# A two-block model on one core: decay factors of the mLSTM by a split row product, four buffers, later ScalarE work, and a key strip ahead of the Hyena transforms

## The reference

```python
logw = F[..., :, None] - F[..., None, :] + ic[..., None, :]
logw = jnp.where(lower, logw, -jnp.inf)
m_t = jnp.maximum(log_inter, jnp.max(logw, axis=-1))
w = jnp.exp(logw - m_t[..., None])
s = jnp.einsum('bhtd,bhsd->bhts', qc, kc) * w
h = num / jnp.maximum(jnp.abs(den), jnp.exp(-m_t))[..., None]
```

## Time and profile before

| | us |
|---|---|
| median of 3 runs | 1810.19 |
| the profiled execution: its time | 1808.34 |
| its span in the trace | 1806.5 |
| TensorE busy with products | 1735.1 (96%) |
| VectorE, ScalarE, GpSimd busy | 877.3, 667.0, 831.5 |

### The profile page before, as it was taken

How to read it: one execution, slowest core, us unless ns; L and a number is a source line. 1 busy time by engine, 2 the same in 40 slices (tenths; PEclk the granted TensorE clock), 3 DMA queues, 4 the chain that set the end, 5 groups by cost and what they waited for, 6 DMA issues and landing times.

```text
span 1806.5 us, 21589 instructions
## 1 busy us (share of the span) xinstructions
PE 1735.1 (96%) x7584; PEld 1398.8 (77%) x7584; DVE 877.3 (49%) x1163; ACT 667.0 (37%) x850; POOL 831.5 (46%) x614
## 2 busy tenths in 40 slices
PE   7999999888998999999999999999999999999996
PEld 4677767776785888888888788888888888888885
DVE  6447666776425371424255767664333343132235
ACT  4434344434423322111124566665333432222222
POOL 4324422467540354444443666565444354444443
PEclk9999999889999999999999999999999999999998
DMA  5112211125220222222222333332222222322222
GB/s 199 59 40 89 70 48 47 70 94 175 85 92 19 97 94 93 93 95 99 97 93 93 108 102 117 105 116 93 93 102 96 94 93 95 103 93 93 104 94 93
DMA packets 47631, 168.60 MB, mean 93 GB/s; under 512 B 5141, under 2 KB 5269, under 8 KB 47322
## 3 DMA queue, kind: packets, MB, share of 16 engines
q1 hardware_dynamic: 46016, 163.75, 26.3%
q10 hardware_dynamic: 1562, 4.13, 0.6%
HBM read 165.76 MB, written 2.10 MB: 93 GB/s over the span
## 4 chain that ended last, share of the span: by engine, by line
PE 42%; issue 21%; POOL 14%; DVE 2%; POOLq 0%; ACT 0%; DMA 0%; DVEq 0%; SPq 0%
PE ps L518 14%; POOL m_w_lo L479 14%; PE ps L519 14%; PE ps L520 14%; DVE m_h L2129 0%; DVE m_ZL L1748 0%; DVE m_qs L1738 0%; DVE m_TM L1822 0%; DVE m_s L1440 0%; DMA m_raw<-in_strips 0%; DVE m_s L1818 0%; POOL m_QL L497 0%; POOLq L487 0%; DVE m_QL L1810 0%; POOLq L485 0%
## 5 line engine op out<-in xcount | busy, mean ns | idle before, releaser
L479 POOL TENSOR_TENSOR m_w_lo<-m_raw,m_w_hi 128x512 fp32r<-128x512 f32 x604 | 816.7, 1374 | 939.1 <-ACT m_w_hi L1003 939.0
L1003 ACT ACTIVATE m_w_hi<-m_raw 128x1024 fp32r<-128x1024 f32 x302 | 318.7, 1057 | 626.7 <-DMA m_raw<-in_strips 626.4
L518 PE MATMUL ps<-m_XH,m_w_hi 128*128 128x512 f32 x1096 | 440.2, 402 | 5.5 <-POOL m_w_lo L479 5.1
L520 PE MATMUL ps<-m_XH,m_w_lo 128*128 128x512 f32 x1096 | 429.4, 392 | 0.0
L519 PE MATMUL ps<-m_XL,m_w_hi 128*128 128x512 f32 x1000 | 392.1, 392 | 0.0
L518 PEld LDWEIGHTS ps<-m_XH,m_w_hi 128*128 128x128 f32 x1096 | 207.6, 189 | 59.5 <-issue 10.4
L520 PEld LDWEIGHTS ps<-m_XH,m_w_lo 128*128 128x128 f32 x1096 | 207.3, 189 | 43.8
L519 PEld LDWEIGHTS ps<-m_XL,m_w_hi 128*128 128x128 f32 x1000 | 189.7, 190 | 40.5 <-issue 2.0
L518 PE MATMUL ps<-m_FH,m_w_hi 128*128 128x512 f32 x432 | 168.3, 390 | 0.3 <-DVE m_FL L1433 0.3
L519 PE MATMUL ps<-m_FL,m_w_hi 128*128 128x512 f32 x432 | 168.2, 389 | 0.0
L520 PE MATMUL ps<-m_FH,m_w_lo 128*128 128x512 f32 x432 | 168.2, 389 | 0.0
(11 more groups left out here) (335 smaller groups left out, 2289.4 us busy)
## 6 DMA issues: line engine op xcount, KB each, us to landing
m_raw<-in_strips SPq DMA_DIRECT2D x302, 512.0 KB, 3.2
m_x_in<-in_x SPq DMA_DIRECT2D x4, 512.0 KB, 11.8
m_x_res<-in_x ACTq DMA_DIRECT2D x1, 2048.0 KB, 8.3
out<-m_h SPq DMA_DIRECT2D x8, 256.0 KB, 2.2
m_decay<-in_decay ACTq DMA_DIRECT2D x1, 1024.0 KB, 10.4
m_memf<-in_mem SPq DMA_DIRECT2D x1, 1024.0 KB, 16.5
m_w<-in_w ACTq DMA_DIRECT2D x1, 512.0 KB, 8.1
m_const<-in_const ACTq DMA_DIRECT2D x1, 256.0 KB, 6.9
```

The lines of the kernel that those rows point to most:

```text
L479: nc.gpsimd.tensor_tensor(w_lo[:, c], raw[:, c], f(w_hi[:, c]), ALU.subtract).then_inc(lo_ready, 1)
L518: pe.matmul(dst, w_hi[:, c], xh, start=first, stop=False)
L520: return pe.matmul(dst, w_lo[:, c], xh, start=False, stop=last)
L1003: act.activation(w_hi[:, c], raw[:, c], ACT.Copy).then_inc(hi_ready, 1)
```

## The change

The row -M is split into a rounded part `gMH` (ScalarE) and the rest `gML` (VectorE), the selector is copied to fp32r (`sel_r`), and `row` becomes two fp32r products instead of one fp32 product. The exponential is one instruction, read from PSUM with a as the bias; where the mask applies its value may exceed 1, and VectorE's product with the triangle becomes a minimum. There are four buffers instead of two. ScalarE's `ahead`, `keep` and `out_squares` come two or three steps later in its order. Column copies and the denominator are done in fewer instructions. The first key strip is stored, loaded and used ahead of the first transform strip, and two key strips' work is placed around `back`.

```diff
-HY_STRIPS = ((S_HY, S_HY + 5, S_HY + 6, S_HY + 7), tuple(range(S_HY + 12, S_HY + 16)))
-K_STRIPS = tuple(range(S_HY + 1, S_HY + 5)) + tuple(range(S_HY + 8, S_HY + 12))
+HY_STRIPS = ((S_HY + 1, S_HY + 5, S_HY + 6, S_HY + 7), tuple(range(S_HY + 12, S_HY + 16)))
+K_STRIPS = (S_HY,) + tuple(range(S_HY + 2, S_HY + 5)) + tuple(range(S_HY + 8, S_HY + 12))
...
+        ex = [s0, s1, at("ex2", T, 116 * KB), at("ex3", T, 118 * KB)]
@@ -676,15 +681,18 @@
-            pe.wait_ge(ld_sel, 16)
+            pe.wait_ge(g_high, 2)
+            pe.wait_ge(g_low, 1)
...
                 if unit:
-                    pe.wait_ge(m_arg, TT * unit)
+                    pe.wait_ge(m_exp, TT * unit)
                 hd, d = divmod(unit, 2)
-                pe.matmul(ps[:, 5, :], sel[0:4, hd * P:(hd + 1) * P], gM[0:4, d * T:(d + 1) * T],
-                          start=True, stop=True).then_inc(m_row, 1)
+                for part in (gMH, gML):
+                    mm = pe.matmul(ps[:, 5, :], sel_r[0:4, hd * P:(hd + 1) * P], part[0:4, d * T:(d + 1) * T],
+                                   start=part is gMH, stop=part is gML)
+                mm.then_inc(m_row, 1)
@@ -803,17 +811,18 @@
+            pe.wait_ge(evac, E_WOUT)
+            pe.wait_ge(mem_ready, KT)
+            keys(0)
             pe.wait_ge(z_ready, 2)
             pe.wait_ge(m_w, STEPS)
-            pe.wait_ge(evac, E_WOUT)
-            pe.wait_ge(mem_ready, KT)
             forward(0, 0)
             forward(0, 1)
-            keys(0)
             keys(1)
             pe.wait_ge(y_ready, 1)
-            back(12, 0)
+            back(12, 0, (0, 1))
             keys(2)
+            back(12, 0, (2, 3))
             keys(3)
@@ -1171,6 +1180,9 @@
             act.activation(gE[0:4, :], gE[0:4, :], ACT.Exp, scale=-1.0).then_inc(g_em, 1)
+            act.activation(gMH[0:4, :], gM[0:4, :], ACT.Copy).then_inc(g_high, 1)
+            act.wait_ge(ld_sel, 16)
+            act.activation(sel_r[0:4, :], sel[0:4, :], ACT.Copy).then_inc(g_high, 1)
             for u in range(1, N_QK):
                 ahead(S_QK + u)
...
+            def behind(n):
+                for m in range(1, N_Z):
+                    if m > 2 and first_step(m * KT + 1) == n - 3:
+                        ahead(S_Z + m)
+                    if m < N_Z - 2 and first_step(m * KT + 16) == n - 4:
+                        keep(m)
+                if n > 2 * TT and n % (2 * TT) == 7:
+                    out_squares(n // (2 * TT) - 1)
...
             for n in range(STEPS):
...
-                if n >= 2:
-                    act.wait_ge(m_w, n - 1)
-                act.activation(e, ps[:, 5, causal(n)], ACT.Relu, bias=misc[:, c:c + 1], scale=-1.0).then_inc(m_arg, 1)
-                act.wait_ge(m_arg, n + 1)
-                act.activation(e, e, ACT.Exp, scale=-1.0).then_inc(m_exp, 1)
-                if n > 2 * TT and n % (2 * TT) == 4:
-                    out_squares(n // (2 * TT) - 1)
-                for m in range(1, N_Z):
-                    if m > 2 and first_step(m * KT + 1) == n - 1:
-                        ahead(S_Z + m)
-                    if m < N_Z - 2 and first_step(m * KT + 16) == n - 1:
-                        keep(m)
+                if n >= 4:
+                    act.wait_ge(m_w, n - 3)
+                act.activation(ex[n % 4][:, causal(n)], ps[:, 5, causal(n)], ACT.Exp, bias=misc[:, c:c + 1]
+                               ).then_inc(m_exp, 1)
+                behind(n)
+            for n in range(STEPS, STEPS + 4):
+                behind(n)
...
+            act.wait_ge(m_w, STEPS)
             keep(N_Z - 2)
@@ -1638,6 +1656,9 @@
             for u in range(1, N_QK):
                 qk_convolved(u)
+                if u == 1:
+                    dve.wait_ge(g_high, 1)
+                    dve.tensor_tensor(gML[g, :], gM[g, :], f(gMH[g, :]), ALU.subtract).then_inc(g_low, 1)
...
-            dve.tensor_scalar(misc[:, 0:32], ps[:, 7, 0:32], -1.0, None, ALU.mult).then_inc(g_colsv, 1)
-            dve.tensor_copy(misc[:, 32:64], ps[:, 7, 32:64]).then_inc(g_colsv, 1)
+            dve.tensor_copy(misc[:, 0:64], ps[:, 7, 0:64]).then_inc(g_colsv, 1)
...
-                ch.add(dve.tensor_tensor(e[:, c], e[:, c], tri[d], ALU.mult))
+                ch.add(dve.tensor_tensor(e[:, c], e[:, c], tri[d], ALU.min))
...
-                ch.add(dve.tensor_copy(den, raw_den))
-                ch.sync()
-                ch.add(dve.scalar_tensor_tensor(den, den, -1.0, den, ALU.mult, ALU.max))
-                ch.sync()
-                ch.add(dve.tensor_tensor(den, den, misc[:, 32 + d * 16 + hd:48 + d * 16:4], ALU.max))
+                ch.add(dve.tensor_tensor(den, raw_den, misc[:, 32 + d * 16 + hd:48 + d * 16:4], ALU.max))
+                ch.sync()
+                ch.add(dve.scalar_tensor_tensor(den, raw_den, -1.0, den, ALU.mult, ALU.max))
...
+                if d == 0:
+                    r = inv.rearrange("p (a c) -> p a c", c=1).to_broadcast([P, TT, P])
+                    ins = dve.tensor_tensor(acc[:].rearrange("p (a c) -> p a c", a=TT), num[:, :, 0:P], r, ALU.mult)
```

More of the change, by code:

```diff
@@ L210, in build @@
         sel = at("sel", 4 * P, 192 * KB + 3584)
+        sel_r = at("sel_r", 4 * P, 192 * KB + 3584, F32R)
+        gMH = at("gMH", 2 * T, 112 * KB, F32R)
+        gML = at("gML", 2 * T, 42 * KB, F32R)
         ZH = at("ZH", TT * T, 136 * KB + 128, F32R)
@@ L354, in build @@
         g_em = sem("g_em")
+        g_high = sem("g_high")
+        g_low = sem("g_low")
         g_cols = sem("g_cols")
@@ L358, in build @@
         m_row = sem("m_row")
-        m_arg = sem("m_arg")
         m_exp = sem("m_exp")
@@ L695, in outputs @@
                 else:
-                    pe.wait_ge(g_colsv, 2)
+                    pe.wait_ge(g_colsv, 1)
                 for tt in range(TT):
@@ L720, in _, with back @@
             z_turn(N_Z - 1)
-            def back(first, count0):
-                for q in range(4):
+            def back(first, count0, qs=range(4)):
+                for q in qs:
                     b = 6 + q % 2
@@ L1195, in _ @@
             ahead(S_Z + 2)
-            act.wait_ge(g_colsv, 2)
+            def behind(n):
[6 more added lines that the diff above has]
+                    out_squares(n // (2 * TT) - 1)
+            act.wait_ge(g_colsv, 1)
             for n in range(STEPS):
@@ L1665, in _ @@
             dve.wait_ge(g_cols, 1)
-            dve.tensor_scalar(misc[:, 0:32], ps[:, 7, 0:32], -1.0, None, ALU.mult).then_inc(g_colsv, 1)
-            dve.tensor_copy(misc[:, 32:64], ps[:, 7, 32:64]).then_inc(g_colsv, 1)
-            dve.wait_ge(g_colsv, 2)
+            dve.tensor_copy(misc[:, 0:64], ps[:, 7, 0:64]).then_inc(g_colsv, 1)
+            dve.wait_ge(g_colsv, 1)
             def weigh(n):
                 unit, d, j = n // TT, n // TT % 2, n % TT
-                e = (s0, s1)[n % 2]
+                e = ex[n % 4]
                 dve.wait_ge(m_exp, n + 1)
                 c = slice(j * P, (j + 1) * P)
-                ch.add(dve.tensor_tensor(e[:, c], e[:, c], tri[d], ALU.mult))
+                ch.add(dve.tensor_tensor(e[:, c], e[:, c], tri[d], ALU.min))
                 ch.sync()
@@ L1699, in outputs @@
                 ch.sync()
-                for tt in range(TT):
-                    c = slice(tt * P, (tt + 1) * P)
-                    r = misc[:, 72 + tt:73 + tt]
-                    if d == 0:
-                        ins = dve.tensor_scalar(acc[:, c], num[:, tt, 0:P], r, None, ALU.mult)
-                    else:
-                        ins = dve.scalar_tensor_tensor(acc[:, c], num[:, tt, 0:P], r, acc[:, c], ALU.mult, ALU.add)
-                    if tt < TT - 1:
-                        ch.add(ins)
+                if d == 0:
+                    r = inv.rearrange("p (a c) -> p a c", c=1).to_broadcast([P, TT, P])
+                    ins = dve.tensor_tensor(acc[:].rearrange("p (a c) -> p a c", a=TT), num[:, :, 0:P], r, ALU.mult)
+                else:
+                    for tt in range(TT):
+                        c = slice(tt * P, (tt + 1) * P)
+                        ins = dve.scalar_tensor_tensor(acc[:, c], num[:, tt, 0:P], misc[:, 72 + tt:73 + tt], acc[:, c],
+                                                       ALU.mult, ALU.add)
+                        if tt < TT - 1:
+                            ch.add(ins)
                 ins.then_inc(m_outused, 1)
@@ L2199 @@
     parts = [pairs(w_in[:, 2560:3584]), spec, strips(gates), strips(w_in[:, 1536:2560]), strips(w_in[:, 0:1536]),
-             order[0:1], keys[0:4], order[1:4], keys[4:8], order, pairs(x["xa_wv"]),
+             keys[0:1], order[0:1], keys[1:4], order[1:4], keys[4:8], order, pairs(x["xa_wv"]),
              strips(x["w_out"]), strips(x["xa_wq"]), strips(x["xa_wo"])]
```

1 line of the change is left out of this document (removed).

## The result

The changed kernel takes 1796.32 us in the median (1794.33 to 1797.25), against 1810.3 (1808.28 to 1814.12) for the kernel before in the same session: ratio 0.9919, 95% interval 0.9900 to 0.9937, 14.0 us faster. Measured again later (e10), the two stood at 1796.2 and 1805.91, ratio 0.9938 (0.9919 to 0.9956). The sign is certain; the size is 14.0 us by the first pair of medians and 9.7 by the second, and the two intervals overlap. The profiled execution of the changed kernel took 1796.37 us, its span is 1794.6.

A forecast was written before the change was run, and what follows sets the result against it. TensorE, busy 96% of the span, bounds the kernel; only its idle or half-clock stretches and own queue can give time. Terms sum to 19.65 us off 1808.34: 1788.7, or 1790.5 against the median; forecast 1790.0, range 1785.5 to 1798.0.

The forecast's parts named there:

- the two holes: mLSTM stretch, rows of units 3 and 7: TensorE half idle, then at half clock, costing 5.47 and 5.18 us.
- VectorE's products collide with GpSimd: Hyena stretch: rival in which these collisions, or a low clock in `forward`, make (f) 0; 1795.8 us, chance 0.07.
- (f): Hyena stretch: `keys(0)` fills TensorE's idle time and VectorE finds its copies ready; 5.3 us gained, ends 3.3 and 6.
- (a): Gates: two new ScalarE copies ahead of a strip's rounding delay TensorE; 1.5 us lost, ends 1.0 and 3.6.
- (b): Row products of units 1 to 7: two fp32r products replace one fp32 product, 0.58 us each; 4.1 us gained.
- two fp32r products of 512 columns take 2 x 0.234: Row products: the split row was priced at 0.47 us against 1.05 for the old one.
- (c): mLSTM unit 0: shorter row and earlier W for the third step; 0.9 us gained, ends 0.6 and 1.2.
- the Relu goes, and W comes some 0.7 us earlier: Unit 0: W of the first step ends about 213.4, limiting the gain to 1.2 us.
- (d): mLSTM stretch: ScalarE's later `ahead` and four buffers remove both holes; 10.65 us gained, lower end 8.
- W of steps 14 and 30: mLSTM stretch: these follow `outputs` and a convolution on VectorE and are late next, with a margin of 1.5 us.
- (e): End of the mLSTM stretch: 0.6 us saved in `outputs(6)` gives only 0.2 us before `z_ready`.
- its rest falls beside the two-input products of VectorE, which costs up to 2: Hyena stretch: GpSimd's rest of strip S_HY + 4, loaded some 9 us earlier, meets VectorE's products; up to 2 us.

The follow-up runs named there:

- e10: The changed kernel measured again, with no edit: 1796.2 us, ratio 0.9938 to the kernel before.
- e6: Changed kernel with ScalarE's two copies behind the next strip's rounding and the `gML` subtraction two convolutions later: 1794.08 us, ratio 0.9941.
- e2: Changed kernel with the row as one fp32 product again, without the two copies and `gML`: 1794.59 us, ratio 0.9935.
- e7: Changed kernel with the rounding of strip S_Z + 5 behind the exponential of step 3, not ahead of step 0's: 1794.0 us, ratio 0.9939.
- e1: Changed kernel with `ahead`, `keep` and the squares back at their old steps, four buffers and single exponential kept: 1800.96 us, ratio 0.9969.
- e8: Changed kernel with two decay buffers instead of four, the later order kept: 1795.83 us, ratio 0.9935.
- e5: Changed kernel with two of ScalarE's strip roundings (S_HY + 4, S_HY + 5) moved in the Hyena stretch: 1793.42 us, ratio 0.9930.
- e3: Changed kernel with ScalarE's two copies behind the next strip's rounding, the `gML` subtraction left in its place: 1795.72 us, ratio 0.9940.
- e9: Changed kernel with the edits of e5, e6 and e7 together: 1791.68 us, ratio 0.9903 to the kernel before.
- e12: e9 with the rounding of strip S_HY + 7 moved behind that of the products of j = 1: 1790.74 us, ratio 0.9900.
- e4: Kernel before with only the Hyena part of the change (strip order, `keys(0)` first, `back` in two halves): 1807.53 us, ratio 1.0000.
- e11: Changed kernel with the Hyena part undone, the mLSTM part alone: 1797.87 us, ratio 0.9955.

## Why the prediction was right, and where its sizes were off

Forecast were 1790.0 us, 1785.5 to 1798.0, faster with 0.93. The time lies inside and the sign is right. The mechanism of the largest term, the two holes, was right too. But the gain was 14.2 us in the segments, and 14.0 and 9.7 in the medians, against a sum of 19.65. The time of 1796.3 is 6.3 us over the forecast and outside the 1787 to 1795 that the prediction gave as its own range without rivals; it is inside the stated range because that one takes in the rivals' prices of 1795.2 to 1795.8. None of the rivals came about as described, so that the time stands beside theirs is chance. The nearest is "VectorE's products collide with GpSimd": it took half of (f) and not all. By the prediction's own terms:

- **(a) Copies: -1.5 forecast, -1.87 measured.** The rounding came 1.5 us later as worked out (169.22 - 166.78 = 2.44 us behind the start of the exponential, against 0.97). TensorE's wait grew by only 1.1, since GpSimd's pair ran 0.3 us shorter; the clock made up the rest (e6). The prediction gave the clock no price here. Its reason why the subtraction does not meet GpSimd does not add up either: from 167.0, at the 2.13 us that it reckoned with, the subtraction ends at 169.1 and not by 168.6. It took 1.21.
- **(b) Rows: +4.1 forecast, about +2.8 measured.** Units 4 and 5, with no hole in them, became 0.41 and 0.38 us shorter, and e2 has the same in units 2 to 6, so 0.4 each for seven, not 0.58. The failing step is "two fp32r products of 512 columns take 2 x 0.234": the rate inside a long run of equal products was taken for a pair of 4-row products that stands alone, and the pair measured 0.65.
- **(c) Unit 0: +0.9 forecast, -0.15 measured.** Unit 0 gained 0.63, at the lower end. Unit 1 became 0.38 longer although its row gave 0.4, by the wait of 0.72 us for the convolution, which comes behind W on VectorE. The step that failed is "the Relu goes, and W comes some 0.7 us earlier". From the first row product to that W it is 213.37 - 206.93 = 6.44 us before and 216.79 - 210.55 = 6.24 after, 0.2 earlier. From the rounding that waits for its DMA to the exponential the time did shrink, by 0.57 (209.37 to 212.31, now 212.94 to 215.31, a table load of 1.28 us inside it both times). But VectorE's minimum then fell beside GpSimd's rest of the same strip (from 214.07, 2.53 long) and took 0.65 us, where the product before had taken 0.29:

```profile
216.10 0.65 DVE L1696 TENSOR_TENSOR m_s<-m_s,m_const 128x128 f32<-128x128 f32 x1 [5.15 <-ACT m_s L1225]
216.79 0.69 DVE L1701 SCALAR_TENSOR_TENSOR m_W<-ps,m_s 128x512 f32<-128x512 f32 x1
```

TensorE in turn came to step 2 sooner, since its clock did not fall at step 0 in this execution (granted clock 1.00 in 211.19 to 213.50 us, against 0.50 in 208 to 210 us before), and waited 1.10 us for W. e7 takes this wait away.

- **(d) Order: +10.65 forecast, 10.8 measured** (units 2, 3, 6 and 7 shortened by 12.4, less four rows of 0.4). This term was priced by the same piece of work without the hole, elsewhere in the trace, so idle time and clock were both in it. e1 shows the mechanism, e8 that the buffers are the smaller part. Its worry, W of steps 14 and 30, shows no wait of TensorE at all.
- **(e) End: +0.2 forecast.** It lies in unit 7 with the second hole and cannot be told from it; the 10.8 of (d) has it in. TensorE waits 1.23 us before `forward`, as expected of `keys(0)`.
- **(f) Hyena: +5.3 forecast, 2.68 measured.** VectorE's idle times of 2.89 and 2.22 us are gone as forecast, the 0.88 stays. In their place stand collisions: +1.08 on the scaling of y, +1.02 on the difference of j = 0 (e5 gives both back, 2.1 us), and +0.90 on the first sum of j = 2 (1.59 us, before 0.69). The step that failed is the step from idle time to gain. The prediction named the cost, "its rest falls beside the two-input products of VectorE, which costs up to 2", and took nothing for it from the 5.3. Taking the 2 would have given 3.3, its own lower bound, and the collisions measured 3.0.

Of its signs, the rows without idle time, the clock of 1.00 in units 3 and 7 and the 1 us before `forward` came. The row products took 0.65 us and not 0.5, TensorE's wait at the gates 4.80 and not 5.2, and before `back` q = 2 a wait of 1.75 us stayed that was to go. One sign of being wrong came too, TensorE waiting for W: 1.10 us at step 2 and 0.29 before `outputs(7)`. Neither made a hole.

The size of (f), and part of that of (c), come from one behaviour. In the changed kernel's Hyena stretch VectorE's operations on 128x512 with two inputs in SBUF took 0.69 us alone and 1.48 to 2.75 when GpSimd was at work; those that read one input from PSUM took 0.68 beside the same work. The longest, and GpSimd's operation that it met, in the timelines of POOL and DVE:

```profile
347.18 2.83 POOL L502 TENSOR_TENSOR m_QL<-m_qs,m_QH 128x1024 fp32r<-128x1024 f32 x1
...
347.80 2.75 DVE L1823 TENSOR_TENSOR m_qs<-m_ftmp 128x512 f32<-128x512 f32 x1
```

The Trainium skill (SBUF — State Buffer, "Who interferes with whom") says that such an operation and a GpSimd instruction reading SBUF share a read port, which the first to issue holds to its end. The trace of the changed kernel agrees: VectorE's operation began 0.62 us after GpSimd's, and if it stood still until that had ended it would take 347.18 + 2.83 - 347.80 + 0.69 = 2.9 us, against 2.75. For (a) the prediction worked 3.6 out of that rule, for the subtraction going first. In the changed kernel it did go first, but had run 0.91 of its 1.21 us before GpSimd began, so at most 0.3 us was blocked. In e3, where it fell into GpSimd's pair, TensorE's wait was 4.47 us instead of the 3.71 of e6.

Shortfall, summed: 0.4 + 1.3 + 1.05 - 0.2 + 0.2 + 2.6 = 5.4 of 19.65 - 14.2 = 5.4 us.

## What to carry to other kernels

An in-order engine's waiting work belongs behind everything that another engine needs soon: count the steps between release and need, and look at the start-up of a loop as well as its body. When a reordering frees an engine's idle time, check what GpSimd does in the new place of each two-input VectorE operation; here moving two roundings returned 2.1 us with no work removed. The rate of a long run of equal products is no price for a short group: the pair took 0.65 us against 0.47.

## What the runs showed of the hardware that was not expected

**The clock at step 0.** The first product of q and k took 1.12 or 1.13 us in nine of the eleven profiled executions with a split row and 1.85 or more in the other two (e9, e12), with the same sequence of transposes and 4-row products ahead of it. With the fp32 row (before, e2, e4) it took 2.07 us or more all three times. The fall costs about 1 us. The row is not the only thing that differs. The last idle time of TensorE, before a turn 2.3 us ahead of the row product, was 0.42 to 0.45 us in seven executions (before, e2, e4, e6, e9, e11, e12), and the clock fell in five of them; it was 0.23 to 0.29 us in the other seven, and the clock fell in none. All three kernels with the fp32 row are among the first seven. So neither the row nor that wait is shown to be the cause: with the wait at its long value and a split row it fell in two of four.

**The same work at two clocks.** In the long rest, which no edit touches, executions differ by whether the clock falls in gaps of the attention part. The windows of the changed kernel and of e10, the same program, in 530 to 540 us:

```profile
530.00:540.00 10.00, 7.16 (x31) 5.96 (x30) 5.46 (x16) 4.88 (x17) 0.00 (x0) 0.85 0.00 0
```

```profile
530.00:540.00 10.00, 7.16 (x36) 6.01 (x35) 4.83 (x12) 3.79 (x16) 1.49 (x2) 1.00 0.16 52
```

Equal busy time, 31 products against 36. The rest took 1350.85 and 1348.64 us in the two. An edit worth 2 us is thus seen in its segment long before it is seen in a median.
